# A two-block layer on one core: two products of the RWKV scan moved from VectorE to GpSimd, with all four engine orders rewritten

## What is computed

```
w_log = -softplus(-(w0[d] + tanh(xw @ w1[d]) @ w2[d])) - 0.5
decay = exp(-exp(w_log))
a     = sigmoid(a0[d] + (xa @ a1[d]) @ a2[d])
kd    = k * (1 + (a - 1) * k_a)
# per head and position t, state 64 x 64:
sa    = state @ (-kk_t)
state = state * decay_t + sa (kk_t * a_t)^T + v_t kd_t^T
out_t = state @ r_t
bonus = sum(r * kd * r_k) * v
```

## Time and profile before

| | us |
|---|---|
| median of 3 runs | 2753.23 |
| range of the runs | 2749.80 to 2753.63 |
| the profiled execution | 2751.32 |
| its span, first to last instruction | 2749.6 |
| the scan, from the fence to the end of iteration 6 | about 1953 to 2323 |

### The profile page before, as it was taken

How to read it: one execution, slowest core, us unless ns; L and a number is a source line. 1 busy time by engine, 2 the same in 40 slices (tenths; PEclk the granted TensorE clock), 3 DMA queues, 4 the chain that set the end, 5 groups by cost and what they waited for, 6 DMA issues and landing times. The chain is left out here.

```text
span 2749.6 us, 50716 instructions
## 1 busy us (share of the span) xinstructions
PE 2659.4 (97%) x21832; PEld 2124.9 (77%) x21832; DVE 1464.3 (53%) x2371; ACT 1223.6 (45%) x2089; POOL 304.0 (11%) x261
## 2 busy tenths in 40 slices
PE   8999999999999999999999999999898989999999
PEld 7887567788888888886488888887676766788887
DVE  4536875743353323444854243497678785652343
ACT  4334764732243222333844233476566765542332
POOL 0023650000000000001200001100222321000000
PEclk9999999999999999999999999999999999999999
DMA  4222002233223232332122223222000001332231
GB/s 188 98 77 93 1 24 92 77 137 108 92 92 110 97 103 96 115 106 82 60 103 95 105 92 102 104 86 93 10 6 12 7 8 67 114 109 92 92 107 62
DMA packets 38717, 227.92 MB, mean 83 GB/s; under 512 B 4400, under 2 KB 8496, under 8 KB 14944
## 3 DMA queue, kind: packets, MB, share of 16 engines
q1 hardware_dynamic: 32720, 201.86, 21.2%
q0 software_dynamic: 5776, 22.82, 2.4%
HBM read 220.41 MB, written 4.26 MB: 82 GB/s over the span
## 5 line engine op out<-in xcount | busy, mean ns | idle before, releaser
L504 DVE TENSOR_TENSOR weights_lo<-ring,weights_hi 128x1024 fp32r<-128x1024 f32 x347 | 428.2, 1235 | 659.9 <-ACT weights_hi L497 654.5
L497 ACT ACTIVATE weights_hi<-ring 128x1024 fp32r<-128x1024 f32 x346 | 363.8, 1053 | 497.4 <-PE bank L729 280.7
L553 PE MATMUL bank<-h_hi,weights_hi 128*128 128x512 f32 x384 | 150.1, 391 | 0.0
L727 PE MATMUL bank<-weights_hi,mlp_p_hi 128*128 128x512 f32 x384 | 149.6, 389 | 0.0
L555 PE MATMUL bank<-h_hi,weights_lo 128*128 128x512 f32 x384 | 149.5, 389 | 0.0
L554 PE MATMUL bank<-h_lo,weights_hi 128*128 128x512 f32 x384 | 149.4, 389 | 0.0
L728 PE MATMUL bank<-weights_lo,mlp_p_hi 128*128 128x512 f32 x384 | 149.4, 389 | 0.0
L729 PE MATMUL bank<-weights_hi,mlp_p_lo 128*128 128x512 f32 x384 | 149.4, 389 | 0.0
L553 PE MATMUL bank<-mlp_h_hi,weights_hi 128*128 128x512 f32 x336 | 130.7, 389 | 0.0
L554 PE MATMUL bank<-mlp_h_lo,weights_hi 128*128 128x512 f32 x336 | 130.7, 389 | 0.0
L555 PE MATMUL bank<-mlp_h_hi,weights_lo 128*128 128x512 f32 x336 | 130.7, 389 | 0.0
(11 more groups left out here) (849 smaller groups left out, 6788.5 us busy)
## 6 DMA issues: line engine op xcount, KB each, us to landing
ring<-in_w_m SPq DMA_DIRECT2D x64, 1024.0 KB, 4.8
ring<-in_w_mb SPq DMA_DIRECT2D x24, 1024.0 KB, 4.7
ring<-in_w_fi SPq DMA_DIRECT2D x22, 1024.0 KB, 4.9
ring<-in_w_fo SPq DMA_DIRECT2D x10, 1024.0 KB, 4.8
ring<-in_w_a SPq DMA_DIRECT2D x7, 1024.0 KB, 4.8
attn_bias<-scratch POOLq DMA_DIRECT2D x16, 448.0 KB, 4.6
ring<-in_w_rg SPq DMA_DIRECT2D x5, 1024.0 KB, 4.9
ring<-in_w_v SPq DMA_DIRECT2D x4, 1024.0 KB, 10.7
```

What stands on the lines that cost most here:

```text
L497: act.e.activation(halves(g, s)[0], raw, ACT.Copy).then_inc(*act.up("act_unit_high", ("high", s)))
L504: lane.e.tensor_tensor(lo, raw, hi.bitcast(F32), ALU.subtract).then_inc(*lane.up(f"{lane.name}_unit_low", ("low", s)))
L553: pe.e.matmul(ps[:, :], hi, xh, start=k == 0, stop=False, skip_group_check=True)
L727: pe.e.matmul(ps[:, :], xh, hi, start=k == 0, stop=False, skip_group_check=True)
```

## The change

The two products kd (`L3067`) and KB (`L3077`) leave `dve_head` and enter `pool_head`: kd as its first step, ahead of the two rho steps, KB as its last. The instructions, their operands and what they wait for stay the same. On DVE the head has 10 steps in place of 12, on POOL 4 in place of 2. The early part of block 0 follows: DVE still takes 7 steps and then what is left of 4, so that BB is now its 7th step; POOL takes all 4. And the four orders are new.

```diff
@@ dve_rwkv_in
     for _ in range(4):
-        next(first)
+        next(first, None)
     end(g, dve, "rwkv_in")
@@ pool_rwkv_in
-    for _ in range(2):
+    for _ in range(4):
         next(first)
     end(g, pool, "rwkv_in")
@@
-ORDER = {"pe": "mmmatamahrararamtmmamhamamahmartmamamamaamamaamaammaama",
-         "act": "tthtrttrrrrtrhthmmthhmmhhmmhmmmmmmhhmmhhmmmmmm",
-         "dve": "ammmmmammamhamatmammaahmamtathrarttmamahahahamamahaahammahahahh",
-         "pool": "mtmmmrthh"}
+ORDER = {"pe": "mmaamtamharararmatmammhammaramahtamammmaammaamaammaamaa",
+         "act": "ttrthttrrrrtrhthmmhhtmmmmhhhmmmmmmmmhmmhhhmmmm",
+         "dve": "mmmaammmammahmatamammaammarartthattammahhahamamahaammahahhaah",
+         "pool": "tmmmmrhhhht"}
@@ dve_head
-    dve.wait_ge(g.at("kd_factor", b))
-    dve.e.tensor_tensor(R.kd, R.kd, both(kT), ALU.mult).then_inc(*dve.up("dve_head", ("kd", b)))
-    yield
     if b:
         for event in (("tokens", b - 1), ("filled", ("products", b - 1, 1, 1, 1))):
             dve.wait_ge(g.at(*event))
     dve.wait_ge(g.at("ka", b))
     dve.wait_ge(g.at("e2", b))
     dve.e.tensor_tensor(R.BB, R.ta, R.sg, ALU.mult).then_inc(*dve.up("dve_head", ("bb", b)))
     yield
-    dve.wait_ge(g.at("kd", b))
-    dve.e.tensor_tensor(R.KB, R.kd, R.sg, ALU.mult).then_inc(*dve.up("dve_head", ("kb", b)))
-    yield
@@ pool_head
+    pool.wait_ge(g.at("kd_factor", b))
+    pool.e.tensor_tensor(R.kd, R.kd, both(R.kT[:, b, :]), ALU.mult).then_inc(*pool.up("pool_head", ("kd", b)))
+    yield
     if b >= 3:
         pool.wait_ge(g.at("advanced", b - 3))
     elif b == 0:
         first_rows_free(g, pool)
     ...
+    if b:
+        for event in (("tokens", b - 1), ("filled", ("products", b - 1, 1, 1, 1))):
+            pool.wait_ge(g.at(*event))
+    pool.wait_ge(g.at("kd", b))
+    pool.wait_ge(g.at("e2", b))
+    pool.e.tensor_tensor(R.KB, R.kd, R.sg, ALU.mult).then_inc(*pool.up("pool_head", ("kb", b)))
+    yield
```

## The result

The changed kernel takes 2777.74 us (median of 3 runs, 2777.22 to 2780.75) against 2753.23: 24.5 us or 1.0% more, ratio 1.0102 with the interval 1.0088 to 1.0115. The sign is the forecast's; the size is 2.7 times the +9.2 of its sum and that of rival C. The profiled execution has a span of 2775.7 us, 26.1 above the one of before. In the table further down, one execution each of h3_orders_norm and k4_kb_after_bb took over 9200 us in a slow state; the ratios leave it out, and without it their medians are 2767.9 and 2748.0.

What follows compares the result with a forecast made beforehand. PE, busy 97% of the span, was taken as the bound, so only its idle time could be won. The terms -4.8 - 0.6 + 6.0 + 6.6 + 2.0 = +9.2 us gave 2762 us, range 2741 to 2778.

Steps and rivals of the forecast that it cites:

- rival C: Both meetings of POOL and DVE cost full price every iteration: +19 us, 2772 and up to 2780; chance 0.20.
- The removal: Two products a block leave DVE, 2.46 us of its 38 an iteration; by itself worth nothing on PE.
- the price on POOL: kd and KB cost about 2.4 us each on POOL, which goes from 13 to some 18 us of 47.
- Step 1: In the advance, Sw on DVE waits for kd on POOL; 1.0 us on PE in six iterations, +6.0 us.
- Step 2: Late in the iteration, BB on DVE waits for KB on POOL; 0.95 us in seven iterations, +6.6 us.
- Step 3: Block 0 before the scan: BB and KB delay the low parts PE waits for; 2.0 us once, bounds 0 to 2.6.
- So the clock plays no part: PE's granted clock is 1.00 (2.4 GHz) in all three iteration rows, so no clock term was counted.
- What the new orders bring: The reordered scan saves PE waits: -4.8 us for masks of prod and -0.6 us for adjacent dependent steps.
- my two terms: First: masks of prod drain banks in time, -4.8 us; second: four adjacent pairs of the advance, 2.01 to 1.93, -0.6 us.
- A: Faster: POOL and DVE exclude each other where PE has cover, Sw running ahead of kd; 2744 us, chance 0.27.
- The last sign of being wrong: DVE's two-input work stands still elsewhere, the cumulative scans against rho, so the loss has another place.
- B: No change: about half of the meetings cost, 0.8 us an iteration, and the orders give it back; 2753, chance 0.18.

Runs made afterwards that it cites:

- h3_orders_norm: g1 with one wait added: bonus_lo on POOL starts only behind the tail's norm product on DVE; 2768.4 us, ratio 1.0059 to the kernel before.
- k4_kb_after_bb: g3 with one wait added: KB on POOL starts only when BB on DVE is through; 2748.2 us, ratio 0.9993 to the kernel before.
- e4: Changed kernel with each moved product replaced by three POOL writes of constants that read nothing, of about the same length; 2767.2 us, ratio 1.0059 to before.
- g1: Kernel before with the new orders, both products still on DVE, kd behind SA6 and KB behind U7; 2770.9 us, ratio 1.0066.
- e2: Kernel before with only the move: both products on POOL, old orders of PE, ACT and DVE; 2757.7 us, ratio 1.0018.
- g3: e2 with block 0's two products back on DVE; 2752.7 us, ratio 0.9995 to the kernel before.
- f1: Changed kernel with Sw issued on DVE behind S of the step before, instead of behind U; 2774.3 us, ratio 1.0081 to the kernel before.
- h4: Kernel before with one wait added: the tail's first norm product on DVE waits until POOL's bonus_lo is through; 2766.9 us, ratio 1.0057.
- h1: g5 with one wait added: bonus_lo on POOL starts only behind the norm product; 2762.3 us, ratio 1.0039 to the kernel before.
- h2: Changed kernel with one wait added: bonus_lo on POOL starts only behind the first norm product; 2773.2 us, ratio 1.0078 to the kernel before.
- g5: g3 with Sw issued on DVE behind S of the step before; 2771.7 us, ratio 1.0070 to the kernel before.
- k1: Changed kernel with ACT's old order put back, all else new; 2821.3 us, ratio 1.0263 to the kernel before.

## Why the forecast was right in sign and wrong in size

**The removal, and the price on POOL: right.** 2.36 and 2.43 us for KB and kd; k4 shows that a DVE with 10 us less to do in seven iterations is worth nothing on PE in the old orders. In the new ones, where PE waits for DVE's queue ahead of ds7, e4 against g1 hints at 6.0 us in seven iterations, which isn't shown beyond the measurement; the forecast has no such gain in its sum.

**Step 1, kd meets Sw: the mechanism right, the size wrong by half.** The forecast had kd from 0.75 us behind as4 and Sw at about 1.25; the trace has as4 at 2226.72 and them 0.80 and 1.18 behind it. It took 1.0 us on PE and got 1.96, its upper bound. The 0.9 us of cover were counted at the wrong step: not x3 but g1, one step ahead of it, waits for the masks, to get its banks, and it doesn't need ACT's copies of xt2 (through at 2230.52). 9.9 us in the five iterations, against 5.0 in the forecast's term; e4 shows that 8.6 of them are kd's reading.

**Step 2, KB meets BB: the meeting there, but most of the wait behind it has another cause.** BB's mean of 1.80 us is under the 2 that I had named as the sign; the clause "with osum as one more POOL instruction behind", which rival C priced, came true as well (the pair's operations have a mean of 899 ns each, 686 before). PE's wait at ds7 is 7.5 us in five iterations. 2.45 of them are the bare trips (5 x 0.49) that the sum has under the orders, which leaves 5.05 against 4.75 in my term. That this comes out so near is luck: in e4, without the reading, 5.7 are left, so both meetings together are worth 1.8, and the rest is e2's late place.

**Step 3, block 0 ahead of the fence: under-sized, and a second effect missed.** Forecast 2.0, bounds 0 to 2.6. From e2 to g3 it is 5.0 us, and 4.5 by the starts of all kernels, beyond the bound. The longer wait is 2.4 us, which the bound had; the other half is the clock. In after, 12 products run at 1.2 GHz, 0.63 us each where before has 0.39; they start 0.43 us apart in place of 0.23, which is 2.4 us. In after itself the scan starts only 2.9 us later, since PE came to this wait 1.6 us earlier than before. Kernels with the same code up to there start the scan up to 1.7 us apart (g3 and k4), so a single pair of traces can't tell 2.9 from 4.5.

**"So the clock plays no part": wrong.** I read it off three iterations at 1.00 in the earlier trace rows. The changed kernel spends 20.4 us at 1.2 GHz where before spends 6.9: 3.1 us more of busy time in the seven iterations and 2.4 in the stage before, together some 5 of the 24.5 us. g1 and h3 have the same sum of iterations, though h3 waits 5.7 us less. It is a second charge beside the waits; which of them bring it isn't shown.

**What the new orders bring, −5.4: wrong in sign, and this is the largest error.** g1 measures +17.5 for the orders with no product moved. Of my two terms the first was half right: the masks of prod give back 1.4 us of 3.0 in five iterations. The second compared four pairs of adjacent steps and overlooked a fifth, ds6 ahead of as7 (0.57 us in the bare case, and seen as 0.57 at 2245.48 ahead of as7); with it this term is +3.4 in place of −0.6. Three more things were put at nothing or left out:
- The norm product against bonus_lo. The walk followed the two moved products and never asked whom POOL's old operations would meet. The new orders let Sw stand still beside POOL's middle (0.96 us), and with that the norm product lost its lead of 0.05 us. ylo has no part in it: the second half of POOL's middle waited for DVE's masks before (0.31 us) as after (0.98), as the forecast said, and f1 has ylo in its new place with the norm product 0.8 us ahead. h4 prices the flip at +15.8 us in the old orders, and h1 at 9.3; in the new ones h2 and h3 measure 4.5 and 2.5, the latter with 5.8 us of clock against 5.7 of idle time won.
- The late e2. "The moves of ACT's steps in the first half of the iteration swap work that PE covers: nothing", and e2's move, in the second half, was priced in step 2 only as a meeting. It puts BB, KB (where it is on DVE) and the pair in front of SA7: SA ahead of ds7 is 7.8 us in five iterations in g1, 5.4 of them above the bare trips, with no product moved.
- The turn of BB and KB waits 2.2 us for kk2's bank (0.4 each) with no such row. It comes with the orders, since g1 has it too.

**The failed step in one line**: the forecast credited the orders with 5.4 us ("I count all as gone", four pairs), and they cost 17.5, by waits for S behind the norm product (+5.2 in five iterations), for SA ahead of ds7 (+7.8) and for kk2's bank (+2.2).

**What PE waited for, changed kernel against before**, five iterations, PE's waits ended by DVE: masks of y3 +9.9, SA at ds7 +7.5, S +4.4, kk2's bank +2.2, masks of prod −1.4, U and the L3085 steps −0.6, together +22.0. Waits on others fell by 5.2 (10.5 to 5.3), which leaves 16.8; the stretches say 16.1.

**The rivals.** C had the right size and a wrong reason: it had both meetings at full price and the orders still giving 5.4. Step 1 did pay its full price; what brought it to +24.5 were the orders. A's premise, that Sw gets in first, failed by 0.38 us. The last sign of being wrong, DVE's two-input work standing still elsewhere, came true with another pair than the one named there. One reading was off: in the earlier trace rows the cumulative scan starts 0.04 us behind rho and not ahead of it; DVE's instruction ahead of the scan, a low part, ran until 1940.25. B's size is that of the move alone (e2 +4.4, g3 0), which the new orders then hid.

**What stays open.** The costs depend on each other: kd and KB's reading is worth 9.7 us of iterations in the new orders (e4), and, without block 0, the whole move nothing in the old ones (g3). The waits of g1 name where the orders' 17.5 us are, but taking one away doesn't give its size back (h3), and which letters of the four strings bring each wasn't separated, since every mixture that ran brought waits of its own. Why the clock falls behind one wait and not behind another isn't shown either.

## What to carry to other kernels

Before an operation that reads SBUF goes to GpSimd, list VectorE's instructions with two inputs in SBUF near its new time, and those behind them; the operation's length there is what each can lose, and a wait on the right one of the two (k4) settles who goes first. Where a move comes with rewritten orders, give each half its own place in the sum, and walk the old operations of the moved-to engine too: the dearest meeting here was between two that nobody had moved, decided by 0.05 us. Before counting cover for a wait, look at the very next product and at the bank that it needs. A clock of 1.00 in a few rows is no promise; ask for it over the whole stretch, before and after: here it fell behind waits of 1.6, 2.0 and 3.95 us.

## What the hardware showed that I had not expected

- A POOL instruction that only writes doesn't hold a DVE instruction with two SBUF inputs: Sw took 0.28 us, 0.40 us into a memset of 0.95 us, and 2.13 beside kd. (The Trainium skill, SBUF — State Buffer, section "Who interferes with whom", has this distinction between GpSimd instructions that read SBUF and those that only write it; the trace agrees, 0.28 us.)
- A DVE instruction with one SBUF input can stand still too, a TENSOR_SCALAR of 128 x 1024. In the changed kernel it takes 0.68 us and once, beside kd, 2.75:

```profile
2025.28 2.36 POOL L3098 TENSOR_TENSOR scan_head<-scan_head,rwkv 128x1024 f32<-128x1024 f32 x1 [14.94 <-ACT scan_head L3023]
2025.44 2.75 DVE L3053 TENSOR_SCALAR scan_head<-scan_head 128x1024 f32<-128x1024 f32 x1
```

- Starts 0.03 us (g5) and 0.05 us (before) apart decide which of the two stands still, and the choice repeats from one iteration to the next: in before the first norm product takes 0.68 us in five iterations of six, in g1 2.75 us in five of six, and in the sixth, with bonus_lo 0.43 us behind, 1.02 and 1.03. It isn't without exception: in k4 one of the six came out the other way (2.04 us at 2092.59).
- PE's clock fell to 1.2 GHz in the middle of work, behind a wait of 2.0 us (after, from 2126.5 to 2128.5), and in h3 behind one of 1.6 us (2020.8 to 2022.4). g1 has a wait of 1.3 us at the same place (2020.6 to 2022.0), and its clock stays at 1.00; whether the 0.3 us decide it isn't shown. In k1, whose waits are longest, it spent 64.9 us of 420 at 1.2 GHz, and was busy for 301.1 us with the work that takes before 283.2.
